# One bank for up to four modulation groups, turned by one set of products

## The reference, and what part of it is touched

```
sh_l, sc_l, g_l = jnp.split(jax.nn.silu(c)     @ w_mod[l] + b_mod[l], 3, axis=-1)
sh_c, sc_c, g_c = jnp.split(jax.nn.silu(c_ctx) @ w_mod[l] + b_mod[l], 3, axis=-1)
hl = xl * (1.0 + sc_l[:, None, :]) + sh_l[:, None, :]
hc = xc * (1.0 + sc_c) + sh_c
```

## Time and profile before

| | us |
|---|---|
| median of 3 runs | 3031.68 |
| lowest, highest | 3028.12, 3031.69 |
| the profiled execution | 3030.58 |
| its span in the trace | 3028.9 |
| TensorE busy in it | 2939.5 (97%) |
| ScalarE busy, VectorE busy | 1309.3, 1815.5 |

### The profile page before, as it was taken

One profiled execution on the slowest core, in us unless ns is written; L12 is line 12 of the kernel. 1 busy time (PEld: TensorE's weight loads), 2 busy tenths in 40 slices (PEclk: granted clock), 3 DMA queues, 4 the chain that ended last, 5 costly groups with the idle time before them and its releaser, 6 DMA issues.

```text
span 3028.9 us, 41364 instructions
## 1 busy us (share of the span) xinstructions
PE 2939.5 (97%) x15214; PEld 2399.3 (79%) x15214; DVE 1815.5 (60%) x2939; ACT 1309.3 (43%) x2003; POOL 99.0 (3%) x156
## 2 busy tenths in 40 slices
PE   7999999999999899999998999999999999999998
PEld 3677777777777688888786888887888888888886
DVE  2254444454644536777785587877877556565564
ACT  2243232333422444444456554545555445454453
POOL 0000010101000001110100000000000000000000
PEclk9999999999999999999999999999999999999999
DMA  9743434343445423443453544444445455555553
GB/s 375 291 165 153 154 153 168 139 168 142 171 166 199 161 94 126 153 142 139 148 182 125 181 166 168 168 166 167 167 180 202 174 187 188 195 188 196 184 194 125
DMA packets 76146, 523.17 MB, mean 173 GB/s; under 512 B 8800, under 2 KB 11360, under 8 KB 13920
## 3 DMA queue, kind: packets, MB, share of 16 engines
q1 hardware_dynamic: 71872, 509.64, 45.6%
q0 software_dynamic: 2688, 8.91, 0.8%
q10 hardware_dynamic: 1440, 2.60, 0.2%
HBM read 519.02 MB, written 2.10 MB: 172 GB/s over the span
## 4 chain that ended last, share of the span: by engine, by line
PE 90%; DVE 5%; ACT 2%; DMA 2%; issue 1%; ACTq 0%; DVEq 0%; SPq 0%; POOLq 0%; POOL 0%
PE bank L1689 24%; PE bank L1692 12%; PE bank L1679 9%; PE bank L1680 9%; PE bank L1681 9%; PE bank L2017 4%; PE bank L2018 4%; PE bank L2019 4%; PE bank L1713 3%; PE bank L1715 2%; PE bank L1714 2%; PE bank L1724 2%; DVE w_lo L1019 2%; DMA raw<-stream 2%; PE bank L1814 1%; PE bank L1849 1%
## 5 line engine op out<-in xcount | busy, mean ns | idle before, releaser
L1019 DVE TENSOR_TENSOR w_lo<-raw,w_hi 128x1024 fp32r<-128x1024 f32 x776 | 938.3, 1224 | 647.2 <-ACT w_hi L556 645.6
L556 ACT ACTIVATE w_hi<-raw 128x1024 fp32r<-128x1024 f32 x776 | 814.8, 1056 | 796.1 <-DMA raw<-stream 345.9
L1679 PE MATMUL bank<-x,w_hi 128*128 128x512 f32 x1152 | 458.0, 398 | 5.4 <-DVE x L1068 3.7
L1680 PE MATMUL bank<-x,w_hi 128*128 128x512 f32 x1152 | 449.6, 390 | 0.0
L1681 PE MATMUL bank<-x,w_lo 128*128 128x512 f32 x1152 | 449.3, 390 | 0.0
L568 ACT ACTIVATE z<-bank 128x512 f32<-128x512 f32 x256 | 153.2, 599 | 432.7 <-PE bank L1692 273.4
L1689 PE MATMUL bank<-xs,w_hi 128*128 128x512 f32 x1280 | 328.2, 398 | 7.4 <-DVE xs L1068 7.4
L1679 PEld LDWEIGHTS bank<-x,w_hi 128*128 128x128 f32 x1152 | 216.6, 188 | 99.6 <-issue 54.3
L1689 PEld LDWEIGHTS bank<-xs,w_hi 128*128 128x128 f32 x1280 | 231.4, 190 | 49.9 <-issue 7.6
L1689 PE MATMUL bank<-mlp_x,w_hi 128*128 128x512 f32 x1024 | 257.1, 393 | 0.0
L1681 PEld LDWEIGHTS bank<-x,w_lo 128*128 128x128 f32 x1152 | 216.7, 188 | 46.5
(11 more groups left out here) (278 smaller groups left out, 3416.0 us busy)
## 6 DMA issues: line engine op xcount, KB each, us to landing
raw<-stream SPq DMA_DIRECT2D x484, 1024.0 KB, 4.8
res<-tokens POOLq DMA_DIRECT2D x8, 512.0 KB, 8.4
work<-tokens POOLq DMA_DIRECT2D x16, 256.0 KB, 7.0
out<-res SPq DMA_DIRECT2D x8, 256.0 KB, 3.4
gain_sb<-final_gain ACTq DMA_DIRECT2D x1, 1024.0 KB, 6.7
table_sb<-tables ACTq DMA_DIRECT2D x1, 640.0 KB, 6.2
pool_sb<-pool_w POOLq DMA_DIRECT2D x8, 64.0 KB, 4.2
work<-lam_in ACTq DMA_DIRECT2D x1, 256.0 KB, 4.6
```

What stands on the lines that cost most here:

```text
L556: own.inc(act.activation(w_hi[:, 2 * unit.parity + g, :], raw[:, unit.slot, g * HALF:(g + 1) * HALF], ACT.Copy), hi_done, 2 * unit.number ...
L1019: own.inc(dve.tensor_tensor(w_lo[:, n, :], raw[:, unit.slot, g * HALF:(g + 1) * HALF], w_hi[:, n, :].bitcast(F32), ALU.subtract), lo_done, ...
L1679: pe.matmul(bank[:, :], hi, operand[:, k, 0, :], start=k == 0, stop=False)
L1680: pe.matmul(bank[:, :], hi, operand[:, k, 1, :], start=False, stop=False)
```

## The change

Groups are gathered in turns. A turn is two groups in each of the four rounds at the start, and four groups in each of the four turns that follow, so there are 8 turns (`TURNS`) for 24 groups. All groups of a turn accumulate in one bank: `cond_x` is 38 columns wide with the two vectors at columns 6 and 7, and the window of 32 columns that a product takes is shifted by two for each group, so that group g of the turn lands in rows 2g and 2g+1 of every strip of 32. ACT's copy, the four products against `chooser` (now eight columns instead of two) and DVE's sums come once for a turn.

```diff
+SHARE = 4
+TURNS = 8
+def mods_before(turn):
+    return 8 * turn if turn < 4 else 32 + 16 * (turn - 4)
+def mod_rows(u):
+    turn = u // 8 if u < 32 else 4 + (u - 32) // 16
+    first, last = mods_before(turn), mods_before(turn + 1) - 1
+    return turn, (u - first) // 4, first, last
-        cond_x = place("cond_x", [KT, SQUARE])
-        chooser = place("chooser", [2])
+        cond_x = place("cond_x", [KT, SQUARE + 2 * (SHARE - 1)])
+        chooser = place("chooser", [2 * SHARE])
+        def product_bank(unit):
+            return att[5] if unit.fixed == PAIRS + 1 else gemm_bank[unit.bank]
...
             for kq in range(4):
-                for b in range(2):
-                    take_mod(2 * kq + b, 0)
-                    if kq and b == 0:
-                        split(Unit(2 * kq - 1))
-                act.wait_ge(mod_done, 2 * kq + 2)
+                if kq:
+                    split(Unit(2 * kq - 1))
+                take_mod(kq, 0, 0)
+                act.wait_ge(mod_done, kq + 1)
...
             for kq in range(4):
-                for b in range(2):
-                    modulation(2 * kq + b, 4 * kq + KT * b, 0)
-                    if kq and b == 0:
-                        split(Unit(2 * kq - 1))
+                if kq:
+                    split(Unit(2 * kq - 1))
+                modulation(kq, 0, [(4 * kq, 0, 1), (KT + 4 * kq, 1, 1)])
...
             def mod_product(u, b):
                 place, q = mod_place(u), u % 4
+                turn, group, first, end = mod_rows(u)
+                window = slice(2 * (SHARE - 1 - group), 2 * (SHARE - 1 - group) + SQUARE)
...
-                    ins = pe.matmul(gemm_bank[b][rows, :], cond_x[:, 4 * q + j, :],
-                                    raw[:, place % RAW_SLOTS, WIDE * j:WIDE * (j + 1)], start=q == 0, stop=q == 3)
+                    ins = pe.matmul(gemm_bank[b][rows, :], cond_x[:, 4 * q + j, window],
+                                    raw[:, place % RAW_SLOTS, WIDE * j:WIDE * (j + 1)], start=u == first, stop=u == end)
...
-                group = 8 + (n - PAIRED) // 4
+                turn = 4 + (n - PAIRED) // 16
                 if n == PAIRED:
                     pe.wait_ge(v_out, 7)
-                elif n % 4 == 2:
-                    pe.wait_ge(mod_done, group)
+                elif (n - PAIRED) % 16 == 0:
+                    pe.wait_ge(mod_done, turn)
                 mod_product(18 + n, 1)
-                if n % 4 == 1:
-                    return lambda: mod_collect(group, 1)
+                if (n - PAIRED) % 16 == 15:
+                    return lambda: mod_collect(turn, 1, 1)
...
             for kq in range(4):
+                if kq:
+                    pe.wait_ge(mod_done, kq)
                 for b in range(2):
-                    if kq + b:
-                        pe.wait_ge(mod_done, 2 * kq + b)
                     for q in range(4):
                         mod_product(8 * kq + 4 * b + q, 0)
                     if kq:
                         value_both(kq - 1, b, 0)
...
-                    mod_collect(2 * kq + b, 0)
+                    if b == 1:
+                        mod_collect(kq, 0, 0)
                     if kq:
                         value_both(kq - 1, b, 1)
```

More of the change, by code:

```diff
@@ L563, in take @@
                 if unit.fixed == PAIRS + 1:
-                    act.wait_ge(mod_done, MOD_GROUPS - 1)
+                    act.wait_ge(mod_done, TURNS - 1)
                 elif not unit.early(V_UNITS[0] + 1):
                     act.wait_ge(z_used, unit.taken + 1 - unit.back)
+                source = product_bank(unit)
                 if gain is None:
-                    last = act.activation(z[:, unit.bank, :], gemm_bank[unit.bank][:, :], ACT.Copy)
+                    last = act.activation(z[:, unit.bank, :], source[:, :], ACT.Copy)
                 else:
@@ L571, in take @@
                         cols = slice(TOK * s, TOK * (s + 1))
-                        last = act.activation(z[:, unit.bank, cols], gemm_bank[unit.bank][:, cols], ACT.Copy,
+                        last = act.activation(z[:, unit.bank, cols], source[:, cols], ACT.Copy,
                                               scale=mod[:, 2 * KT + gain, s:s + 1])
@@ L630, in slot, with take_mod @@
                     after()
-            def take_mod(group, b):
-                act.wait_ge(mod_mm, 4 * group + 4)
-                own.inc(act.activation(z[:, b, :], gemm_bank[b][:, :], ACT.Copy), modz_full, group + 1)
+            def take_mod(turn, b, row):
+                act.wait_ge(mod_mm, mods_before(turn + 1))
+                own.inc(act.activation(z[:, row, :], gemm_bank[b][:, :], ACT.Copy), modz_full, turn + 1)
             def round_even(k):
@@ L727, in after @@
                                 late_tile(k)
-                    if l == 0 and unit.fixed > PAIRED and unit.fixed % 4 == 1:
-                        take_mod(8 + (unit.fixed - PAIRED) // 4, 1)
+                    if l == 0 and unit.fixed > PAIRED and (unit.fixed - PAIRED) % 16 == 15:
+                        take_mod(4 + (unit.fixed - PAIRED) // 16, 1, 1)
                     slot(unit, gate=gate, wide=wide, after=after)
@@ L764, in layer_out @@
                 for k in range(KT):
-                    if l == 0 and k % 4 == 1:
-                        take_mod(19 + k // 4, 1)
+                    if l == 0 and k == 1:
+                        take_mod(TURNS - 2, 1, 1)
                     if k == KT - 1:
@@ L1049, in _ @@
             own.wait_own()
-            own.inc(dve.tensor_tensor(cond_x[:, :, 0:2], cond_sb[:], cond_e[:], ALU.mult), cond_full, 1)
+            own.inc(dve.tensor_tensor(cond_x[:, :, 2 * (SHARE - 1):2 * SHARE], cond_sb[:], cond_e[:], ALU.mult), cond_full, 1)
             dve.wait_ge(vec_in, 16)
@@ L1055, in _, with later_modulation, modulation @@
             own.wait_own()
[L1056 to L1063, removed]
+            def later_modulation(turn):
+                modulation(turn, 1, [(mods_before(turn), 0, SHARE)])
+            def modulation(turn, b, places):
+                dve.wait_ge(mod_sum, turn + 1)
+                sums_at = gemm_bank[b][:, 0:8 * SHARE].rearrange("p (c g s) -> p g c s", c=4, s=2)
+                for m, first, n in places:
+                    for s in range(2):
+                        target = mod[:, m:m + 4 * n, s].rearrange("p (g c) -> p g c", c=4)
+                        bias = vec[:, VEC_COLS["b_mod"] + m:VEC_COLS["b_mod"] + m + 4 * n]
+                        last = dve.tensor_tensor(target, sums_at[:, first:first + n, :, s],
+                                                 bias.rearrange("p (g c) -> p g c", c=4), ALU.add)
+                own.inc(last, mod_done, turn + 1)
             def rest_x(n, k, source, target, t):
@@ L1252, in after @@
                                 rest_x(3, k, res[:, k, ycols], x_late, TOK)
-                    if l == 0 and unit.fixed > PAIRED and unit.fixed % 4 == 1:
+                    if l == 0 and unit.fixed > PAIRED and (unit.fixed - PAIRED) % 16 == 15:
                         inner = before
                         def before():
-                            group = 8 + (unit.fixed - PAIRED) // 4
-                            modulation(group, 4 * group, 1)
+                            later_modulation(4 + (unit.fixed - PAIRED) // 16)
                             inner()
@@ L1303, in before @@
                     def before():
-                        if l == 0 and k % 4 == 1:
-                            group = 19 + k // 4
-                            modulation(group, 4 * group, 1)
+                        if l == 0 and k == 1:
+                            later_modulation(TURNS - 2)
                         if k >= 2:
@@ L1653, in product @@
             def product(unit, mode, phase, operand, halfway=None):
-                bank = gemm_bank[unit.bank]
+                bank = product_bank(unit)
                 for g in range(2):
@@ L2125, in shape_tables @@
     chooser = np.zeros((P, P))
-    for s in range(2):
+    for s in range(2 * SHARE):
         chooser[s::SQUARE, s] = 1.0
```

29 lines of the change are left out of this document (13 added, 16 removed).

## The result

| | before | changed |
|---|---|---|
| median, us | 3031.69 (5 runs) | 3014.79 (5 runs) |
| lowest, highest | 3028.12, 3033.33 | 3013.13, 3017.49 |
| the profiled execution, its span | 3030.58, 3028.9 | 3014.74, 3013.0 |

The ratio is 0.995 with a 95% interval of 0.9938 to 0.9961: 12 to 19 us less. The forecast was 3016.3 in a range of 3010.5 to 3021.5. First the page of the changed kernel, to be put beside the earlier trace rows.

A forecast was written before the change was run, and what follows sets the result against it. TensorE was taken as the bound where it is full, a loop of latencies at the start. 11.4 us from interleaved collects plus 4.0 from the start, 15.4, gave a median of 3016.3 us; range 3010.5 to 3021.5.

The forecast's parts named there:

- Interleaved collects: Stretch where TensorE is full: twelve of 15 collects go at 0.95 us each, 11.4 us gained.
- Wider collect, ACT, DVE, mod products at 0: Eight-column collects, fewer ACT copies and DVE sums, and shifted windows of the mod products were each taken as worth 0.
- Rival C: Mod products become bound by weight loads with shifted windows: slower, up to 75 us less the 15.4, 3091; chance 0.03.
- The start, 4.0 us: Rounds 0 to 3: gains of 2.30, 1.38 and 0.95 us less 0.6 for longer DVE sums; bounds -0.6 and 16.5.
- Round 0 at 0: Start: first collect and its wait go, but the stream sets the time until about 50 us; worth 0, bounds 0 and 1.
- Round 1: Start: one collect gone, 0.95 us, and an earlier slot ends an idle 1.35 us; sum 2.30.
- Round 2: Start: one collect gone, 0.95 us, and a 0.43 us wait ends; sum 1.38; waits of 1.05 and 2.56 us stay.
- rival A: The stream sets the start: it gives nothing and longer sums cost 0.6 us; 3020.9 us, chance 0.12.
- Round 3's 4.75 us: Start: the wait, 4.68 us in before, stays; only the collect's 0.95 us is gained, nothing from the clock.
- the loop of latencies: Start: units come late because slots free late, through collect, modulation, x tiles and even unit's split, not because transfer engines are full.
- The rest: Span outside start and interleaved part: the last group's swapped banks and moved unit were taken at 0.

The follow-up runs named there:

- later turns alone: Kernel before's start, one group a turn, with four groups a turn behind it; 3018.14 us, ratio to before 0.9946 to 0.9973.
- bare turns: Changed kernel with twelve bare sets of four products put back where collects went, without ACT's copy and DVE's sums; 3025.10 us.
- start alone: Changed kernel's start, with one group a turn behind it as before; 3028.20 us, ratio to before 0.9978 to 0.9996.
- odd split first: Kernel before, with only the odd value unit's split moved ahead of the first bank copy and modulation sum in rounds 1 to 3; 3029.04 us.
- fill: Changed kernel with products of zeros in TensorE's waits, five in round 1 and nine in round 3; 3015.65 us.
- both fill and early split: Changed kernel with the even value unit split ahead of the modulation sums in rounds 1 to 3, plus five products of zeros in round 1; 3004.14 us.
- early even split: Changed kernel with the even value unit also split ahead of the modulation sums in rounds 1 to 3, on ACT and DVE; 3008.03 us.
- changed again: The changed kernel itself, unaltered, traced once more; 3014.49 us in one run.
- round 0 too: Changed kernel with the even value unit split ahead of the modulation sums in rounds 0 to 3, plus five products of zeros in round 1; 3007.42 us.

## Why the prediction was right, and where it was not

**Interleaved collects, 11.4 us: right.** Measured 11.52, and 11.39 with the later turns alone, 11.11 for the bare products. The reading from the cadence gave the price; the medians of single instructions would have doubled it.

**Wider collect, ACT, DVE, mod products at 0: right.** The four sums of a round take 0.37 us for the pair's 0.23, as taken. Rival C is out: eight products still take 1.06 us in the start's free rows. The estimate from the Trainium skill, page "SBUF — State Buffer", section "Door 1: The DMA port swizzle", an eighth more per unaligned load, does not show: the loads of the mod products have a median of 109 ns and a mean of 112 in both traces, where an eighth on half of them would have made the mean 119. Whether the loads felt it beneath their idle time no run here shows.

**The start, 4.0 us: near in size, in part by luck, and wrong in some steps.** The profile gave 5.18, but the mean of the four traces of this start is 231.37, against 233.90 and 234.18 of before's: 2.7 us; the medians of the start alone say 3.7. Single traces against before's 233.90 say anything from 0.65 to 5.18. The steps:

- Round 0 at 0: no trace shows a gain, and a loss is not shown either. The changed kernel's profile has its collect at the lower level (1.88 us for eight; 1.41 in before) and place 12 issued at 37.98 us for 36.52. But with before's own round 0 the collect takes 1.06 us in the later turns alone and 1.87 in the odd split first, with place 12 at 36.24 and 37.50; with the changed one it takes 1.06 to 1.88, with place 12 at 36.24 to 37.98.
- Round 1, 2.30 less 0.16: the wait for u15 went as said. But u12 began 1.35 us later than in before, since value unit 0 ran its first products at the lower level (0.63 us for 0.39). I had taken the clock as unchanged there. The changed kernel is not what lowered it: u12 begins at 57.25 us in the later turns alone, which have before's start, and at 57.88 in the odd split first. Of the eight traces without a fill only that of before has these products at the upper level from the first on; the rows that the prediction was read from were the lucky ones. What gave the lower clock is open.
- Round 2: the 0.43 us at u23 went. The prediction said that u19's wait stays "in substance" because place 22 hangs on the collect. It stays because the stream brings u19 at about 77 us: an earlier issue does not bring it sooner, and ten of the eleven traces have it between 75.3 and 77.9, with issues from 65.3 to 72.6. That is rival A, true of this round. In three of them it took 4.8 to 4.9 us from issue to use, in another, with the same neighbours in the queue, 7.3 us (79.89, the bare turns). Why so different is open.
- Behind u19 the changed kernel had luck: through its waits of 0.73, 1.40 and 1.43 us the clock stayed up, and u20 began at 89.04. In the start-only trace, with a wait of 4.18 us, it fell, and u20 began at 92.82. The length of the waits alone does not decide it: the odd split first has waits of 0.79, 1.20 and 1.43 us and its clock fell during u19 (1.51 us), while with both fill and early split it stayed up through one of 2.67. What does is open.
- Round 3's 4.75 us: the wait stayed as forecast, and its reason, the loop of latencies, is shown by the early even split.

**The rest.** I took it as unmoved. Single traces lie in two places, at 2002.4 to 2003.8 and at 2000.3 to 2001.0. Two of them in the same stretch, first the changed kernel, then the later turns alone:

```profile
2350.00:2420.00 70.00, 66.74 (x325) 56.49 (x324) 36.30 (x52) 30.67 (x37) 0.00 (x0) 0.95 0.48 171
```

```profile
2353.00:2423.00 70.00, 66.74 (x338) 56.77 (x337) 37.81 (x56) 32.37 (x39) 0.00 (x0) 1.00 0.50 182
```

With the same busy time of TensorE the granted clock is 0.95 in the one and 1.00 in the other. All six traces of the upper place have such a fall of the clock there and none of the five of the lower. It accounts for the surplus of the later turns over their 11.39 us in the trace (13.5 of span); the changed kernel's 0.8 us more lies within the spread of the upper place. In the same way the interleaved part is 0.9 to 1.1 us longer in the three traces in which the clock is down for 6.8 us instead of 3.4 near 800 us (changed again, odd split first, round 0 too).

Whether the change has a part in where the rest lies is not settled. All three traces with 15 collects in the interleaved part (before, start only, odd split first) are in the upper place, five of the eight with turns of four groups in the lower. By medians the bare turns, which put TensorE's twelve sets back, are 3.1 us below the start alone, while their interleaved parts differ by only 0.45. If both kinds of kernel fell into the upper place equally often, three of three would still come out by chance once in eight (estimate: six of the eleven are there). So up to some 2 us of the 16.9 by medians may be a term that the sum of 15.4 does not have.

## What to carry to other kernels

Where TensorE is full, the worth of a removed burst of small products is its place in the cadence, from the burst's start to the next stage less the undisturbed steps, and it came back whole here. Where the engine waits for a stream, ask of each wait apart whether the slot or the transfer is late: issue the load sooner and look whether the data come sooner. And such a stage wants more than one trace, of the kernel before too: the start of one program came out anywhere within 4.5 us, and the clock behind its waits differed between traces with nearly the same waits. Moving a split ahead of a wait that it does not need won more there (6.8 us) than this change did in the start (2.7 to 3.7).

## What the runs showed of the hardware

- The same transfers, issued at the same distances (place 22, then 23 and 24 within 0.9 us), bring the first one to use 4.8 us after its issue in one trace (before) and 7.3 in another (bare turns).
- Products whose moving operand is zeros go with the upper level of the clock as others do: with five of them between the mod units of round 1, u11 takes 1.06 us (fill) and 1.07 (both), in the changed kernel 1.94. In all three kernels with the fill the first product of value unit 0 takes 0.50 us, in seven of the eight without it 0.80.
- The granted clock of a stretch ahead of the first recorded change is not to be trusted: the start-only trace gives 1.00 from 25 to 50 us, while its mod units take 1.93 and 1.94 us there. The durations of like products tell the level.
